# Decoder layer on one Trainium2 core: one block's top-256 found by dropping 128 keys, the embedding norm's affine pass of chunk 1 moved to GpSimd, logits stored with the sign changed

## Chip, cores, metric

One core of one Trainium2 chip. The metric is the device time of one launch in microseconds; of the kernel before there are three timed runs and one profiled execution.

## What is computed

One layer of a decoder over 1024 tokens of width 1024, float32. The parts that matter here:

```python
x = layer_norm(x, emb_ln_g, emb_ln_b)          # gain and bias per column: the affine pass
proj = x @ w_in                                # pool channels 512 | q 512 | latent 128 | indexer q, k, w
pooled = trailing means over 2, 4, 8, 16 tokens, minus the token
score[t, s] = sum_h w[t, h] * relu(iq[t, h] . ik[s]), causal
idx = top_k(score, 256)                        # per token
logits = q_lat . c[idx] / 8 + bias[t - s];  p = softmax(logits) per head
x = layer_norm(2 ** 0.25 * x + concat(pool, attn) @ w_o)
x = layer_norm(2 ** 0.25 * x + relu(x @ w_up) ** 2 @ w_down)
```

The selected keys are not gathered: a mask of 0 (selected) and -1e30 is added to the logits of all keys up to the block's end. The softmax needs the maximum of a row before exp.

## The kernel before

Tokens come in two chunks of 512, each of four blocks of 128. Weights are streamed in units of 128 x 1024 float32 through four ring slots (`wring`); ACT copies each to a rounded part `whi`, GpSimd or DVE subtracts to get `wlo` (`split_lo`, L413), two slots each, and PE multiplies three passes per product. The order of work on each engine is written out by hand, with semaphores; nothing reorders it. PE runs projections of chunk 0, projections of chunk 1, attention 0, output projection 0, feed-forward 0, then attention 1, output projection 1, feed-forward 1. `rows` holds the token rows of one chunk, so the rows of the other chunk wait in DRAM (`spilld`).

**Selection.** Blocks 2 and 3 (384 and 512 keys) are selected together by `select_pair`, on DVE, while PE projects chunk 1: 32 rounds of MAX8 (the eight largest of a row) and MATCH_REPLACE8 (replace them by TAKEN, -3e38), for both blocks in turn. `mask_of` (L878, L879) turns what was taken into the mask. Blocks 0 and 1 have no more than 256 keys. Blocks 4 to 7 are selected later one by one, in feed-forward 0 (`select`, L912 to L919, 640 to 1024 keys).

**Pooling.** `pooling` (L544 to L563) makes four groups of channels from `uT`; in chunk 1 PE's order is q0 q1 q2 u0 u1 u2 po0 u3 po1 q3 po2 po3, and each `po` waits for one group. The last of them is PE's last work before attention 0; GpSimd's head masks for attention 0 wait for it too.

**The affine pass.** `emb_gains` multiplies `rows` by the gain and adds the bias, two passes of 128 x 1024 per block (L656, L657). Chunk 0's is on GpSimd at the start. Chunk 1's is on DVE: three blocks between the groups of pooling, the fourth in step 16 of attention 0. SP then writes the rows to DRAM, loads the next gains, and loads chunk 0's rows for the residual.

**Attention.** A step is one head of one block. DVE adds mask and logits from PSUM and reduces to the row's maximum (L932), negates it (L936), ACT takes exp with that as the bias, PE transposes, ACT and DVE split the transposed probabilities (L948), PE multiplies with the latents. Two buffers alternate between steps.

**Feed-forward 0.** Four groups of 16 units: units 0 to 7 are columns of `w_up`, units 8 to 15 pairs of `w_down` rows. GpSimd does all `wlo` splits, each two units ahead of PE, and in units 0 to 7 the low part of the activations; before its splits at units 11 and 15 it adds four pieces of y to `rows` (`add_y`, L748). SP issues each unit's load when the split of four units earlier is done. Behind feed-forward 0 SP loads four `w_o` units, ACT makes the first two rounded parts at the last two units of the last group, GpSimd makes their low parts after its last `add_y`, and then the head masks of attention 1.

## Time and profile before

| | us |
|---|---|
| runs, median of 3 | 1287.44 (1285.87 to 1287.86) |
| profiled execution, its own time | 1285.83 |
| its span, first to last instruction | 1283.9 |
| PE busy | 1213.2 (94% of the span) |
| DVE busy | 857.3 (67%) |
| ACT busy | 557.8 (43%) |
| GpSimd busy | 494.6 (39%) |
| mean granted clock of TensorE | 0.984 |

A row of the profile names the engine, the line, the operation, `out<-in` and the shapes; in a time order the first number is the start in us from the span's start, the second the duration, and a bracket at the end gives the idle time of the engine before it and what ended that. PE's busy time includes modelled ends of matmuls that overlap. PE is TensorE, DVE VectorE, ACT ScalarE, POOL GpSimd, SP the engine whose queue issues the DMAs.

### The profile page before, as it was taken

The page shows a single profiled execution, that of the slowest core. Times are in us where ns is not written, and L with a number is a line of the kernel's source. Part 1 is how long each engine was busy: PE and PEld are TensorE (multiplying, and loading weights), DVE is VectorE, ACT ScalarE, POOL GpSimd, SP SyncE. Part 2 cuts the span into 40 slices and gives each one's busy share as a digit, 9 for nine tenths or more (in the row PEclk, how much of TensorE's full clock was granted, in tenths as well). Part 3 has the DMA queues.
Part 4 walks back from the last instruction along what each step waited for, and adds up shares of the span by engine and source line. Part 5 has one row for each costly group of instructions (what it writes and reads, how often), then busy time and mean ns, then how long its engine had stood idle before and what let it go on. Part 6 is the DMA issues. An engine that isn't in the chain of part 4 may idle for free.

```text
span 1283.9 us, 17048 instructions
## 1 busy us (share of the span) xinstructions
PE 1213.2 (94%) x5639; PEld 975.5 (76%) x5639; DVE 857.3 (67%) x1326; ACT 557.8 (43%) x943; POOL 494.6 (39%) x362
## 2 busy tenths in 40 slices
PE   4999899699989999999999999989899999999997
PEld 2787686577868878778778779878788888888886
DVE  7677999775966888888888768956532232332336
ACT  3444653576346334344244276662243342442440
POOL 5534674432526666666675652302101101102002
PEclk9899999899989999999999999999899999999999
DMA  6631232031302332233232300224022332333241
GB/s 199 223 98 50 67 98 99 17 148 34 99 17 66 98 99 85 95 98 94 85 98 98 114 2 18 84 98 132 17 95 87 98 98 87 92 98 98 85 127 68
DMA packets 125728, 114.38 MB, mean 89 GB/s; under 512 B 5661, under 2 KB 99434, under 8 KB 125674
## 3 DMA queue, kind: packets, MB, share of 16 engines
q1 hardware_dynamic: 125674, 113.67, 28.7%
q8 instruction: 33, 0.54, 0.2%
q14 instruction: 21, 0.17, 0.0%
HBM read 105.25 MB, written 8.40 MB: 89 GB/s over the span
## 4 chain that ended last, share of the span: by engine, by line
PE 75%; DVE 13%; issue 6%; ACT 2%; POOL 2%; DMA 1%; DVEq 1%; POOLq 0%; SPq 0%; ACTq 0%
PE g_bank L1465 13%; PE g_bank L1467 13%; PE g_bank L1466 13%; PE wide L1465 10%; PE wide L1467 10%; PE wide L1466 10%; PE g_bank L1430 3%; DVE logit L932 1%; DVE score L871 1%; DVE win L548 1%; PE wide L1570 1%; DVE probs_lo L948 1%; DVE work L898 1%; PE wide L1529 1%; PE wide L1530 1%
## 5 line engine op out<-in xcount | busy, mean ns | idle before, releaser
L413 POOL TENSOR_TENSOR wlo<-wring,whi 128x1024 fp32r<-128x1024 f32 (+1 forms) x94 | 230.1, 2449 | 263.3 <-ACT whi L1348 140.8
L1465 PE MATMUL g_bank<-xhi,whi 128*128 128x512 f32 (+1 forms) x736 | 297.3, 404 | 6.1 <-DVE xlo L578 2.7
L1466 PE MATMUL g_bank<-xlo,whi 128*128 128x512 f32 (+1 forms) x736 | 293.1, 398 | 0.0
L1467 PE MATMUL g_bank<-xhi,wlo 128*128 128x512 f32 (+1 forms) x736 | 293.0, 398 | 0.0
L1348 ACT ACTIVATE whi<-wring 128x1024 fp32r<-128x1024 f32 x120 | 127.1, 1059 | 361.7 <-PE g_bank L1467 179.9
L413 DVE TENSOR_TENSOR wlo<-wring,whi 128x1024 fp32r<-128x1024 f32 (+1 forms) x66 | 88.1, 1336 | 218.7 <-ACT whi L1348 217.5
L1465 PE MATMUL wide<-whi,hhi 128*128 128x512 f32 x480 | 190.0, 396 | 0.0
L1466 PE MATMUL wide<-wlo,hhi 128*128 128x512 f32 x480 | 189.6, 395 | 0.0
L1467 PE MATMUL wide<-whi,hlo 128*128 128x512 f32 x480 | 189.6, 395 | 0.0
L1465 PEld LDWEIGHTS g_bank<-xhi,whi 128*128 128x128 f32 (+1 forms) x736 | 138.9, 189 | 45.0 <-issue 5.1
L748 POOL TENSOR_TENSOR rows<-rows,y_stage 128x512 f32<-128x512 f32 x56 | 72.7, 1317 | 249.2 <-ACT y_stage L1338 247.9
L1467 PEld LDWEIGHTS g_bank<-xhi,wlo 128*128 128x128 f32 (+1 forms) x736 | 138.6, 188 | 34.9 <-issue 0.9
L1466 PEld LDWEIGHTS g_bank<-xlo,whi 128*128 128x128 f32 (+1 forms) x736 | 139.1, 189 | 34.1 <-issue 2.0
L916 DVE MAX8 top<-work 128x8 f32<-128x640 f32 (+3 forms) x128 | 131.7, 1029 | 18.7 <-DVE work L919 0.2
L919 DVE MATCH_REPLACE8 work<-top,work 128x640 f32<-128x640 f32 (+3 forms) x128 | 129.2, 1010 | 0.0
L1465 PEld LDWEIGHTS wide<-whi,hhi 128*128 128x128 f32 x480 | 90.0, 187 | 23.0 <-POOL wlo L413 1.2
L1467 PEld LDWEIGHTS wide<-whi,hlo 128*128 128x128 f32 x480 | 90.0, 187 | 22.1
L1466 PEld LDWEIGHTS wide<-wlo,hhi 128*128 128x128 f32 x480 | 90.0, 187 | 21.8
L1161 ACT ACTIVATE whi<-wring 128x1024 fp32r<-128x1024 f32 (+1 forms) x40 | 41.6, 1041 | 118.3 <-PE g_bank L1467 104.0
L739 POOL TENSOR_TENSOR mask<-score,near_bias 128x256 f32<-128x256 f32 (+1 forms) x64 | 44.7, 700 | 78.4 <-DVE row_max L932 68.5
L871 DVE SCALAR_TENSOR_TENSOR score<-relu_sb,idx_w,score 128x384 f32<-128x384 f32 (+5 forms) x42 | 56.7, 1363 | 27.1 <-ACT relu_sb L1227 26.0
L932 DVE CUSTOM_DVE_ANT_0 logit<-wide,mask 128x128 f32<-128x128 f32 (+7 forms) x64 | 48.3, 755 | 31.6 <-PE g_bank L1430 25.5
(200 smaller groups left out, 1932.3 us busy)
## 6 DMA issues: line engine op xcount, KB each, us to landing
wring<-in_w_up SPq DMA_DIRECT2D x64, 512.0 KB, 4.0
wring<-in_w_down SPq DMA_DIRECT2D x64, 512.0 KB, 3.7
wring<-in_w_in SPq DMA_DIRECT2D x26, 512.0 KB, 3.7
wring<-in_w_o SPq DMA_DIRECT2D x16, 512.0 KB, 3.7
rows<-in_x SPq DMA_DIRECT2D x8, 512.0 KB, 5.2
normalized_rows<-rows SPq DMA_DIRECT2D x8, 512.0 KB, 4.0
rows<-normalized_rows SPq DMA_DIRECT2D x8, 512.0 KB, 6.6
out<-rows SPq DMA_DIRECT2D x7, 512.0 KB, 2.6
```

The lines of the kernel that those rows point to most:

```text
L413: eng.tensor_tensor(parts_of(name, lo_tile(name)), parts_of(name, wring[n % 4]), parts_of(name, hi_tile(name)).bitcast(F32), ALU.subtract) ...
L739: pool.tensor_tensor(mask[:, m % 2, length - near:length], score[:, i % CB, length - near:length], near_bias[:, h, NEAR - near:NEAR], ALU. ...
L748: pool.tensor_tensor(piece, piece, y_stage[:, b, :], ALU.add).then_inc(y_added, 1)
L871: nc.vector.scalar_tensor_tensor(out=s, in0=relu_sb[:, n % 2, 0:length], scalar=idx_w[:, i, h:h + 1], in1=s, op0=ALU.mult, op1=ALU.add)\
L916: nc.vector.max(top8[:, 0, :], w).then_inc(topk_steps, 1)
L919: nc.vector.match_replace(w, top8[:, 0, :], w, TAKEN).then_inc(topk_steps, 1)
L932: nc.vector.tensor_tensor_reduce(logit[:, m % 2, 0:length], wide[m % 2][:, 0:length], mask[:, m % 2, 0:length], 1.0, TAKEN, ALU.add, ALU.m ...
L1161: nc.scalar.activation(parts_of(name, hi_tile(name)), parts_of(name, wring[n % 4]), ACT.Copy).then_inc(hi_ready, 1)
L1348: nc.scalar.activation(whi[(R[("mlp", c, 0)] + j) % 2][:, :], wring[(first + j + 2) % 4][:, :], ACT.Copy)\
L1465: nc.tensor.matmul(out_ap, w_hi, m_hi, start=first, stop=False)
L1466: nc.tensor.matmul(out_ap, w_hi, m_lo, start=False, stop=False)
L1467: return nc.tensor.matmul(out_ap, w_lo, m_hi, start=False, stop=last)
```

## The change

Three parts; none changes what is computed.

1. `select_pair`: block 2 has 384 keys, of which 256 are selected, so 128 are dropped. Its scores are copied negated and in reverse order of keys, 16 rounds take the 128 smallest, and one operation turns those into the mask. Block 3 goes on alone for 16 more rounds. In `pooling` a scaling and a subtraction become one operation.
2. The affine pass of chunk 1 leaves DVE. SP writes the normalized rows to DRAM at once; during feed-forward 0 it loads one block per group into `emb_stage` (which lies, with `emb_rows_g`, where the indexer keys and two parked `w_o` units have been), GpSimd makes the two passes on it before its split at unit 13, and SP writes the block back. The loops over groups of SP and GpSimd in feed-forward 0 are written out.
3. The masked logits are stored negated, `-(logit + mask)`, with a running minimum, which is the negated maximum itself; exp gets the scale -1.

```diff
         key_lo = part("key_lo", 100.25, [P, S], F32R)
+        emb_rows_g = part("emb_rows_g", 88.25, [P, 2, D])
...
                 sp.wait_ge(*LO[units[first - 1]])
+                    with sp.Fori(0, GROUPS) as g:
+                        for j in range(GUNITS):
+                            load_mlp_unit(c, g, j)
+                    return
+                for g in range(GROUPS):
                     for j in range(GUNITS):
...
+                        load_mlp_unit(c, g, j)
+                        if (g, j) == (0, 8):
+
+                            sp.wait_ge(proj_full, 2 * CB)
+                            sp.wait_ge(relu_ready, 48)
+                            sp.dma_start(emb_rows_g[:, 0, :], emb_ln_g.rearrange("(o d) -> o d", o=1).to_broadcast([P, D])).then_inc(emb_gain_in, 16)
+                            sp.dma_start(emb_rows_g[:, 1, :], emb_ln_b.rearrange("(o d) -> o d", o=1).to_broadcast([P, D])).then_inc(emb_gain_in, 16)
+                        if j == 8:
+                            load_stage(g)
+                        if j == 4 and g:
+                            store_stage(g - 1)
+                store_stage(CB - 1)
+
+            def load_stage(b):
+
+                sp.wait_ge(spilled, 16 * (NB + max(b - 1, 0)))
+                sp.dma_start(emb_stage[:, b % 2, :], spilld[CB + b]).then_inc(stage_in, 16)
+
+            def store_stage(b):
+
+                sp.wait_ge(emb_rows, CB + b + 1)
+                sp.dma_start(spilld[CB + b], emb_stage[:, b % 2, :]).then_inc(spilled, 16)
...
             for b in range(CB):
-                sp.wait_ge(emb_rows, CB + b + 1)
+                sp.wait_ge(xhat_ready, CB + b + 1)
                 sp.dma_start(spilld[CB + b], rows[:, b, :]).then_inc(spilled, 16)
+            sp.wait_ge(emb_rows, CB)
             load_gains(ln1_g, ln1_b)
             sp.wait_ge(spilled, 16 * NB)
+
+            sp.wait_ge(g_full, EV[("xT", 1, KT - 1)])
             for b in range(CB):
                 sp.dma_start(rows[:, b, :], spilld[b]).then_inc(rows_in, 16)
             load_units(units[U[("wo", 0, 1, 0)]:U[("mlp", 0, 0)]])
...
             sp.wait_ge(stored, 16 * CB)
+            sp.wait_ge(spilled, 16 * (NB + CB))
             for b in range(CB):
                 sp.dma_start(rows[:, b, :], spilld[CB + b]).then_inc(rows_in, 16)
...
                 if g >= 2:
 
                     eng.wait_ge(g_full, EV[("po", c, g - 2)])
-                link(eng.tensor_scalar(done, src[:, HIST:HIST + CHUNK], 1.0 / w, None, ALU.mult))
                 if c == 0:
 
                     link(eng.tensor_tensor(done[:, 0:w - 1], src[:, HIST:HIST + w - 1], recip_count[:, 0:w - 1], ALU.mult))
                     link(eng.tensor_copy(hist[:, g, :], u[:, CHUNK:CHUNK + HIST]))
-                eng.tensor_tensor(done, done, u[:, HIST:HIST + CHUNK], ALU.subtract).then_inc(pooled_ready, 1)
+                    link(eng.tensor_tensor(done[:, 0:w - 1], done[:, 0:w - 1], u[:, HIST:HIST + w - 1], ALU.subtract))
+                at = w - 1 if c == 0 else 0
+                eng.scalar_tensor_tensor(out=done[:, at:CHUNK], in0=src[:, HIST + at:HIST + CHUNK], scalar=1.0 / w,
+                                         in1=u[:, HIST + at:HIST + CHUNK], op0=ALU.mult, op1=ALU.subtract)\
+                    .then_inc(pooled_ready, 1)
...
+            def emb_gains():
+
+                pool.wait_ge(gains_in, 32)
+                pool.wait_ge(g_full, EV[("xT", 0, KT - 1)])
+                for b in range(CB):
+                    link(pool.tensor_tensor(rows[:, b, :], rows[:, b, :], gains[:, 0, :], ALU.mult))
+                    pool.tensor_tensor(rows[:, b, :], rows[:, b, :], gains[:, 1, :], ALU.add).then_inc(emb_rows, 1)
+
+            def staged_gains(b):
+
+                pool.wait_ge(emb_gain_in, 32)
+                pool.wait_ge(stage_in, 16 * (b + 1))
+                row = emb_stage[:, b % 2, :]
+                link(pool.tensor_tensor(row, row, emb_rows_g[:, 0, :], ALU.mult))
+                pool.tensor_tensor(row, row, emb_rows_g[:, 1, :], ALU.add).then_inc(emb_rows, 1)
...
                     if j in (GT + 3, GT + 7):
                         add_y(c, g, (j - GT) // 4)
+                    if j == GT + 5:
+                        staged_gains(g)
...
-            mlp_lo(pool, 0, 0, False, first_group)
-            with pool.Fori(1, GROUPS - 1) as g:
-                mlp_lo(pool, 0, g, False, add_at(0, g))
-            mlp_lo(pool, 0, GROUPS - 1, True, add_at(0, GROUPS - 1))
+            for g in range(GROUPS):
+                mlp_lo(pool, 0, g, g == GROUPS - 1, first_group if g == 0 else add_at(0, g))
...
             def select_pair():
 
                 w = [work[:, 0:3 * P], work[:, 3 * P:7 * P]]
+                drop, rounds = P // 8, TOPK // 8
 
                 dve.wait_ge(diag_masked, 2)
-                for e in range(2):
-                    nc.vector.tensor_copy(w[e], score[:, 2 + e, 0:(3 + e) * P]).then_inc(topk_steps, 1)
-                with dve.Fori(0, TOPK // 8) as r:
+                nc.vector.tensor_scalar(w[0], score[:, 2, 3 * P - 1::-1], -1.0, None, ALU.mult).then_inc(topk_steps, 1)
+                nc.vector.tensor_copy(w[1], score[:, 3, 0:4 * P]).then_inc(topk_steps, 1)
+                with dve.Fori(0, drop) as r:
                     for e in range(2):
 
                         dve.wait_ge(topk_steps, 4 * r + (1 + e))
@@ -896,9 +947,19 @@
                         dve.wait_ge(topk_steps, 4 * r + (3 + e))
                         dve.sem_inc(topk_turn, 1)
                         nc.vector.match_replace(w[e], top8[:, e, :], w[e], TAKEN).then_inc(topk_steps, 1)
-                dve.wait_ge(topk_steps, 2 + 4 * (TOPK // 8))
-                for e in range(2):
-                    mask_of(2 + e, w[e])
+
+                dve.wait_ge(topk_steps, 2 + 4 * drop)
+                s = score[:, 2, 3 * P - 1::-1]
+                nc.vector.tensor_scalar(s, w[0], TAKEN, NEG, ALU.is_equal, ALU.mult).then_inc(mask_ready, 1)
+                with dve.Fori(0, rounds - drop) as r:
+                    dve.wait_ge(topk_steps, 2 * r + (2 + 4 * drop))
+                    dve.sem_inc(topk_turn, 1)
+                    nc.vector.max(top8[:, 1, :], w[1]).then_inc(topk_steps, 1)
+                    dve.wait_ge(topk_steps, 2 * r + (3 + 4 * drop))
+                    dve.sem_inc(topk_turn, 1)
+                    nc.vector.match_replace(w[1], top8[:, 1, :], w[1], TAKEN).then_inc(topk_steps, 1)
+                dve.wait_ge(topk_steps, PAIR_STEPS)
+                mask_of(3, w[1])
...
                 nc.vector.tensor_tensor_reduce(logit[:, m % 2, 0:length], wide[m % 2][:, 0:length],
-                                               mask[:, m % 2, 0:length], 1.0, TAKEN, ALU.add, ALU.max,
-                                               row_max[:, m % 2:m % 2 + 1]).then_inc(masked, 1)
-                dve.wait_ge(masked, m + 1)
-                nc.vector.tensor_scalar(neg_max[:, m % 2:m % 2 + 1], row_max[:, m % 2:m % 2 + 1], -1.0, None,
-                                        ALU.mult).then_inc(neg_max_ready, 1)
+                                               mask[:, m % 2, 0:length], -1.0, -TAKEN, ALU.add, ALU.min,
+                                               neg_max[:, m % 2:m % 2 + 1]).then_inc(masked, 1)
...
                         mask_logits(step)
-                    if step == 16:
-
-                        next(gained)
...
             select_pair()
-            gained = emb_gains(dve, 1, chain)
             for g in pooling(dve, 1, chain):
-                if g < 3:
-                    next(gained)
+                pass
             dve.wait_ge(masks01_ready, 2)
             attention(0)
...
-                act.wait_ge(neg_max_ready, m + 1)
+                act.wait_ge(masked, m + 1)
                 p = logit[:, m % 2, 0:(i + 1) * P]
-                nc.scalar.activation(p, p, ACT.Exp, bias=neg_max[:, m % 2:m % 2 + 1],
+                nc.scalar.activation(p, p, ACT.Exp, scale=-1.0, bias=neg_max[:, m % 2:m % 2 + 1],
                                      accum_out=exp_sum[:, i % 2, h:h + 1]).then_inc(exp_ready, 1)
...
             act.wait_ge(y_added, CB + 8 * GROUPS)
+
+            act.wait_ge(spilled, 16 * (NB + CB))
             attention(1)
```

DVE from the selection to the second group of pooling in chunk 1 (`win` is a partial window sum), before:

```order
L898 MATCH_REPLACE work<-top,work 128x512
L888 REGISTER_ALU
L888 COMPARE_AND_BRANCH
L878 TENSOR_TENSOR score<-work,score 128x384
L879 TENSOR_SCALAR score<-score 128x384
L878 TENSOR_TENSOR score<-work,score 128x512
L879 TENSOR_SCALAR score<-score 128x512
L544 COPY uT<-hist 128x16
L548 TENSOR_TENSOR win<-uT 128x527
L558 TENSOR_SCALAR pooledT<-win 128x512
L563 TENSOR_TENSOR pooledT<-pooledT,uT 128x512
L656 TENSOR_TENSOR rows<-rows,gains 128x1024
```

and after the change, from the end of the paired loop:

```order
L939 COMPARE_AND_BRANCH
L953 TENSOR_SCALAR score<-work 128x384
L954 UNCONDITIONAL_BRANCH
L954 ISA
L957 MAX top<-work 128x8
L958 REGISTER_ALU
L960 MATCH_REPLACE work<-top,work 128x512
L954 REGISTER_ALU
L954 COMPARE_AND_BRANCH
L928 TENSOR_TENSOR score<-work,score 128x512
L929 TENSOR_SCALAR score<-score 128x512
L582 COPY uT<-hist 128x16
```

A second loop of 512 keys alone has come in, and the passes on `rows` that stood between the groups are gone.

POOL in the second half of a group of feed-forward 0 after the change (L415 are the splits, L797 the additions of y, L788 and L789 the staged passes):

```order
L797 TENSOR_TENSOR rows<-rows,y_stage 128x512 x4
L415 TENSOR_TENSOR wlo<-wring,whi 128x1024 x2
L788 TENSOR_TENSOR emb_stage<-emb_stage,emb_rows_g 128x1024
L789 TENSOR_TENSOR emb_stage<-emb_stage,emb_rows_g 128x1024
L415 TENSOR_TENSOR wlo<-wring,whi 128x1024 x2
L797 TENSOR_TENSOR rows<-rows,y_stage 128x512 x4
```

Before, four splits stood between the two sets of additions, with nothing among them.

SP at the end of feed-forward 0 after the change:

```order
L499 DMA wring3<-in_w_down 128x2x512 [waits lo_pool]
L483 DMA normalized_rows<-emb_stage_117 128x1024 [waits emb_rows]
L437 DMA wring0<-in_w_o 128x2x512 [waits lo_pool]
L437 DMA wring1<-in_w_o 128x2x512 [waits lo_pool]
L437 DMA wring2<-in_w_o 128x2x512 [waits lo_pool]
L437 DMA wring3<-in_w_o 128x2x512 [waits lo_pool]
```

The store with its wait for GpSimd's last staged pass is new; the loads of `w_o` stood right behind the last unit's load.

## Rows read from the trace of the kernel before

**Rows 1.** Busy us (x instructions) of each engine in a stretch, granted clock, DMA share, GB/s

```profile
core 0: us, PE busy (x) PEld busy (x) DVE busy (x) ACT busy (x) POOL busy (x), PEclk, DMA share, GB/s
...
203.00:234.00 31.00, 20.19 (x79) 14.15 (x78) 29.79 (x37) 8.06 (x11) 11.40 (x4) 0.88 0.27 95
...
365.00:738.00 373.00, 373.00 (x1606) 299.46 (x1604) 310.13 (x417) 152.32 (x210) 231.72 (x129) 1.00 0.29 90
...
768.00:857.00 89.00, 83.66 (x607) 76.45 (x605) 72.48 (x145) 57.62 (x125) 21.56 (x33) 1.00 0.19 72
```

**Rows 2.** Waits of PE, 200 to 236 us: total, times, longest

```profile
PE g_bank L1551 <- DVE pooledT L563: 9.1, 2, 8.2
```

**Rows 3.** The chain of waits, 120 to 262 us: start, duration, what

```profile
203.82 0.43 DVE score L879
...
233.81 2.09 PE g_bank L1551 x2
```

**Rows 4.** DVE in order of time, 120 to 260 us

```profile
130.40 1.14 DVE L893 MAX8 top<-work 128x8 f32<-128x384 f32 x2
...
199.85 1.16 DVE L893 MAX8 top<-work 128x8 f32<-128x384 f32 x2
...
210.78 2.37 DVE L544 COPY uT<-hist 128x16 f32<-128x16 f32 x1
...
224.30 3.37 DVE L656 TENSOR_TENSOR rows<-rows,gains 128x1024 f32<-128x1024 f32 x1
...
228.84 0.17 DVE L544 COPY uT<-hist 128x16 f32<-128x16 f32 x1
```

**Rows 5.** DVE in the rounds of block 4 (640 keys)

```profile
408.10 0.83 DVE L916 MAX8 top<-work 128x8 f32<-128x640 f32 x1
...
410.13 0.83 DVE L916 MAX8 top<-work 128x8 f32<-128x640 f32 x1 [0.15 <-DVE work L919]
```

**Rows 6.** ACT and POOL in order of time, at the last group of pooling

```profile
216.30 0.58 ACT L1128 ACTIVATE uT<-g_bank 128x512 f32<-128x512 f32 x1
...
216.47 2.94 POOL L413 TENSOR_TENSOR wlo<-wring,whi 128x1024 fp32r<-128x1024 f32 x1 [3.35 <-ACT whi L1161]
```

**Rows 7.** POOL, DVE and ACT in a group of feed-forward 0

```profile
542.63 2.41 POOL L413 TENSOR_TENSOR wlo<-wring,whi 128x1024 fp32r<-128x1024 f32 x1 [1.32 <-ACT whi L1348]
548.40 3.20 POOL L413 TENSOR_TENSOR wlo<-wring,whi 128x1024 fp32r<-128x1024 f32 x1 [3.36 <-ACT whi L1348]
...
548.38 0.96 DVE L878 TENSOR_TENSOR score<-work,score 128x768 f32<-128x768 f32 x1
...
552.94 1.06 ACT L1348 ACTIVATE whi<-wring 128x1024 fp32r<-128x1024 f32 x1 [4.62 <-PE wide L1467]
```

**Rows 8.** PE in order of time, step 16 of attention 0

```profile
258.79 0.52 PE L1430 MATMUL g_bank<-ident,logit 128*128 128x128 f32 x3 [1.71 <-DVE probs_lo L948]
```

**Rows 9.** DVE and ACT in order of time, first step of attention 0

```profile
236.82 0.08 DVE L932 DVE_READ_ACCUMULATOR2_ANT row_max<- 128x1 f32 x1
236.94 0.15 DVE L936 TENSOR_SCALAR neg_max<-row_max 128x1 f32<-128x1 f32 x1
...
237.13 0.40 ACT L1259 ACTIVATE logit<-logit,neg_max 128x128 f32<-128x128 f32 x1 [0.53 <-DVE neg_max L936]
```

**Rows 10.** The chain of waits in both attentions: pieces of the negation

```profile
236.94 0.17 DVE neg_max L936
...
850.46 0.15 DVE neg_max L936
```

**Rows 11.** DVE: the first mask operation at the end of three selections

```profile
472.28 2.27 DVE L878 TENSOR_TENSOR score<-work,score 128x640 f32<-128x640 f32 x1
...
633.92 2.08 DVE L878 TENSOR_TENSOR score<-work,score 128x896 f32<-128x896 f32 x1
...
727.18 1.22 DVE L878 TENSOR_TENSOR score<-work,score 128x1024 f32<-128x1024 f32 x1
```

**Rows 12.** ACT at the end of feed-forward 0; landing of a burst of four loads

```profile
732.90 1.06 ACT L1161 ACTIVATE whi<-wring 128x1024 fp32r<-128x1024 f32 x1 [4.62 <-PE wide L1467]
...
DMA to landing us min/median/max: 5.1/6.5/8.8
```

More of the change, by code:

```diff
@@ L299, in layer @@
         emb_rows = sem("emb_rows")
+        emb_gain_in = sem("emb_gain_in")
+        stage_in = sem("stage_in")
         x1_rows = sem("x1_rows")
@@ new lines, in load_mlp, with load_mlp_unit @@
+                store_stage(CB - 1)
[5 more added lines that the diff above has]
+                sp.dma_start(spilld[CB + b], emb_stage[:, b % 2, :]).then_inc(spilled, 16)
+            def load_mlp_unit(c, g, j):
+                first = U[("mlp", c, 0)]
+                sem_lo, lo_base = LO[("mlp", c, 0)]
+                slot = (first + j) % 4
+                sp.wait_ge(sem_lo, g * GUNITS + (lo_base - 1 + j - 4 + 1))
+                if j < GT:
+                    src = wupd[:, :, bass.ds(g * (GT * P) + j * P, P)]
+                    dst = k_columns(wring[slot])
+                else:
+                    nh, u = divmod(j - GT, 4)
+                    src = wdownd[:, bass.ds(g * GT + 2 * u, 2), nh * 512:nh * 512 + 512]
+                    dst = k_pairs(wring[slot])
+                sp.dma_start(dst, src).then_inc(ring_in[slot], 16)
@@ L649, in mlp_lo @@
                         .then_inc(h_lo_ready[c], 1)
-        def emb_gains(eng, c, link):
-            eng.wait_ge(gains_in, 32)
-            eng.wait_ge(g_full, EV[("xT", c, KT - 1)])
-            for b in range(CB):
-                link(eng.tensor_tensor(rows[:, b, :], rows[:, b, :], gains[:, 0, :], ALU.mult))
-                eng.tensor_tensor(rows[:, b, :], rows[:, b, :], gains[:, 1, :], ALU.add).then_inc(emb_rows, 1)
-                yield b
         @block.gpsimd
@@ L754, in _ @@
             inverse_std(EMB0)
-            for b in emb_gains(pool, 0, link):
-                pass
+            emb_gains()
             latents_inverse_rms(0)
@@ L908, in select @@
                 rounds = TOPK // 8
-                first = 2 + 4 * rounds + (2 * rounds + 1) * (i - 4)
+                first = PAIR_STEPS + (2 * rounds + 1) * (i - 4)
                 dve.wait_ge(diag_masked, i - 1)
```

16 lines of the change are left out of this document (3 added, 13 removed).

## Prediction

> **What bounds the kernel now.** I read the busy time by stretches first [rows 1]. From 365 to 738 us (chunk 0's feed-forward) PE is busy for all 373 us: nothing taken off another engine shortens it, and only something that makes PE wait can change it. Time can be gained where PE has holes: 203 to 234 us (20.19 busy of 31, granted clock 0.88) and the attentions. Busy time overstates PE in the attentions, since the ends of matmuls are modelled and short ones overlap, so there I go by the chain and not by the busy share.
>
> The waits of PE name the first hole: 9.1 us for `pooledT`, 8.2 of it in one piece [rows 2]. The chain gives the order of events: the pair's selection ends with a mask operation at 203.82 + 0.43, and the last pool product (two matmuls) starts at 233.81, takes 2.09 us at the clock that had fallen behind the hole, and opens attention 0 [rows 3]. DVE's order of time shows what lies between: the selection runs from 130.40, its last round starts at 199.85 (31 rounds in 69.45 us, 2.24 each), and then pooling alternates with the gain and bias passes on `rows`. Two DVE operations there are far longer than their size: the gain pass of 3.37 us at 224.30, and a copy of 16 columns that takes 2.37 us at 210.78 and 0.17 at 228.84 [rows 4]. The long ones met a split on GpSimd.
>
> **The selection.** The first 16 rounds stay pairs: 16 x 2.24 = 35.8 us. The other 16 handle 512 keys alone. No row shows a round of 512 alone. From above it is bounded by the round of 640, 410.13 - 408.10 = 2.03 us [rows 5], from below by half of a pair round, 1.12. A fifth of the elements of MAX8 (0.83) and of the equally long replacement goes, 0.33, so I take 1.70: it has the same two waits as the 640 round. Sum 27.2. The two first operations (before: until 130.40) I leave as they are; a reversed read can cost or save there, by at most the 4 us that they take together. With some 0.5 for one mask and 1.1 for the other the selection ends at 130.4 + 35.8 + 27.2 + 1.6 = 195.0 instead of 204.2, 9 us earlier (4 to 18).
>
> **Pooling of chunk 1.** Its last group needs `u3`, which ACT writes from 216.30 to 216.88; GpSimd started a split at 216.47 [rows 6], and the copy into `uT` waits for its end as the one at 210.78 did: with the 2.4 of an undisturbed split [rows 7], until 218.9. Then the group itself: from 228.84 [rows 4] to 233.81 it took 4.97, of which one pass over 512 (some 0.5) is fused away: 4.5. The product can start at 218.9 + 4.5 = 223.4, against 233.81: 10.4 earlier, and without a hole of 8 us PE stays at 2.4 GHz instead of 1.2, so it takes about 1.1 instead of 2.09. **Term A: -11.4** (-9.5 to -13). Selection and passes don't add. With the passes gone, DVE pools three groups and idles before `u3` even if the selection ended at 204.2. With the passes kept and the selection short, the last pass would still hide mostly in this same slack. The dropped rounds thus buy slack rather than time, and an error in my round of 1.70 costs nothing up to 8 us.
>
> **The passes in attention 0.** The fourth block's two passes stand in step 16, and behind them PE idles 1.71 us for `probs_lo` [rows 8]; loops around it lose a little too. **Term B: -1.9** (0 to -3).
>
> **The sign change.** Before: the accumulator is read from 236.82 to 236.90, the negation follows at 236.94 and takes 0.15, exp starts at 237.13 [rows 9]. With exp behind the read directly, at the 0.04 that it now has behind the negation, 0.19 of latency goes per head step. It counts where the negation is on the chain: 8 pieces in 234 to 298 us and 10 in 747 to 862, the first and the last of the 18 in [rows 10]. **Term C: -18 x 0.19 = -3.4** (-0.5 if neighbouring paths are as long, -8 if DVE's own time counts in the second attention too). I price the main instruction with scale -1 and min like the one before, having no row of it.
>
> **The staged passes in the feed-forward.** This is work that PE could come to wait for. GpSimd's split 14 runs from 542.63 to 545.04 and split 15 starts at 548.40 [rows 7]. Two passes over 1024 columns, priced as splits, 2.4 each, do not fit into 3.36 us: 545.04 + 4.9 = 549.9, and split 15 ends at 552.3. PE needs it when unit 14 ends, which is when ACT's next split starts, 552.94. Margin 0.6 us, where nothing else is in the way. But DVE starts an operation with two SBUF inputs in this gap, the mask at 548.38, and beside it the split took 3.20 instead of 2.40 [rows 7]. The groups are alike and some 90 us apart, so I look where each selection ends [rows 11]. In the second group the mask of 0.96 gets between: 0.96 - 0.6 = 0.4 over the margin. In the third the mask at 633.92 lasts to 636.0, 0.9 into the gap, and its scaling and the next copy (0.6 and 0.7 by their sizes) follow: 2.2 - 0.6 = 1.6. In the fourth the mask at 727.18 takes 1.22 and its scaling 0.6: 1.2. In the first the mask comes at 472.28, outside. **Term D: +3.1** (0 to +6).
>
> The Trainium skill (SBUF — State Buffer, Who interferes with whom) says that the pair of ports shared by DVE and GpSimd is held for a whole instruction by whichever starts first, and that a DVE instruction with two SBUF inputs contends with a GpSimd one that reads SBUF. By it, if GpSimd's second pass always starts before the waiting DVE operation, D would be 0 and the sum 3.1 less; the disturbed rows agree with the lock, none shows who wins between two GpSimd passes.
>
> **The queue of SP.** Its four added loads, four stores and two gain loads fall into the feed-forward, where a weight load is issued four units ahead; the earlier spill and reload of `rows` likewise come long before their use. I price these at nothing, by the cover of four units of 548.40 - 542.63 = 5.8 us [rows 7]. One is different: the store of stage 3 now stands ahead of the four loads of `w_o`. It waits for the fourth staged pass, which by the pattern above ends 3.0 before unit 14 does (732.90 here [rows 12]) and 1.2 later for the mask: at about 731.1. With half a us for the issue of the store, the first `w_o` unit lands at 731.6 + 5.1 = 736.7 or later, by the fastest of a burst of four (5.1/6.5/8.8 us, [rows 12]). ACT wants it at 732.90, or 1.2 later with D, and waits 2.6 us. Queued behind that are the evacuations of y, two of which are paced by PE anyway; GpSimd's additions, its two splits and the first masks of attention 1 come behind them. ACT catches up, GpSimd does not quite. **Term E: +1.0** (0 to +4).
>
> **Sum.** -11.4 - 1.9 - 3.4 + 3.1 + 1.0 = -12.6. The profiled execution would go from 1285.83 to 1273.2 (span 1271.3). The median lies 1.6 above it; I subtract the same from it: 1287.44 - 12.6 = **1274.8 us**. A measurement tells 0.2%, 2.6 us, from no change.
>
> **Rivals.**
> 1. *The staged passes always fit, and GpSimd is late nowhere*: D and E are 0. For it: 0.6 of margin and GpSimd's idle time of 3.3 us. Against: the mask in the gap. 1287.4 - 16.7 = 1270.7. Chance 0.27.
> 2. *DVE's own time counts throughout attention 1*: C is 8, not 3.4. For it: DVE is busy 72.48 of 89 us there [rows 1]. 1274.8 - 4.6 = 1270.2. Chance 0.12.
> 3. *The selection does not shorten as thought, because reversed access is slow*: only beyond 8 us does it reach PE. With 8 us spare and 12 lost it would be 1278.8. Chance 0.04.
> 4. *The other side: the staged passes throw GpSimd out of step in each group.* If both passes and the splits behind them wait for DVE throughout, split 15 is late by the whole 4.9, and the cost decides the sign from 3.9 us per group on (12.6 + 3.1 over four groups): 4 x 4.9 = 19.6 instead of D, 1274.8 + 16.5 = 1291.3. For it: no cover but 3.36 us. Against: DVE's selection rounds in this stage don't lengthen splits. Chance 0.04.
>
> My forecast has the remaining 0.53. Range: from 1268.5 (rival 1 with A 2.2 better) to 1280.5 (C at 0.8 and D and E together 3.1 dearer: -12.6 + 2.6 + 3.1 = -6.9). Rival 4 and several worst ends together lie outside. Faster 0.93, same 0.03, slower 0.04.
>
> **What would show it.** The last pool product near 223.4; DVE idle before it, with the selection ended by 196; ACT's exp 0.04 behind the accumulator read; no DVE pass in attention 0; splits of GpSimd behind the staged passes ending 0 to 1.6 us after PE wants them; the first `w_o` split of ACT some 3 us behind the end of unit 14. It is wrong if PE stops for over 2 us in any group of the feed-forward, if the pool product comes after 226, or if attention 1 begins with a hole much longer than before.

## The result, and the profile after

| | before | changed |
|---|---|---|
| median of the runs side by side, us | 1287.57 (4 runs, 1285.87 to 1287.86) | 1273.15 (4 runs, 1271.55 to 1274.00) |
| ratio, 95% interval | | 0.989, 0.9878 to 0.9902 |
| profiled execution, us (span) | 1285.83 (1283.9) | 1274.00 (1272.2) |

The change brings 14.4 us by the medians; 1274.8 us was predicted, which was a change of 12.6. The profiled executions differ by 11.8, the spans by 11.7. That gap between 14.4 and 11.7 matters below.

The stretches of [rows 1] in the kernel after, the last two moved to where the same work now lies:

```profile
core 0: us, PE busy (x) PEld busy (x) DVE busy (x) ACT busy (x) POOL busy (x), PEclk, DMA share, GB/s
203.00:234.00 31.00, 28.55 (x123) 21.66 (x122) 19.84 (x46) 15.02 (x40) 14.81 (x15) 0.94 0.69 252
353.00:726.00 373.00, 372.29 (x1602) 298.93 (x1601) 315.04 (x417) 151.15 (x209) 248.75 (x134) 1.00 0.32 100
757.00:846.00 89.00, 85.22 (x625) 78.60 (x624) 71.70 (x126) 59.78 (x129) 21.66 (x33) 1.00 0.19 72
```

PE has 28.55 us of work in the first stretch instead of 20.19 and DVE 10 less; in the feed-forward PE loses 0.7; GpSimd carries 17 us more there. The waits of PE from 200 to 236 us, where [rows 2] showed 9.1:

```profile
PE wide L1625 <- DVE neg_max L993: 1.5, 1, 1.5
PE g_bank L1606 <- DVE pooledT L602: 0.7, 1, 0.7
```

DVE, GpSimd and PE around the last pooling group (order of time; they answer to rows 3, 4 and 6):

```profile
196.18 0.43 DVE L929 TENSOR_SCALAR score<-score 128x512 f32<-128x512 f32 x1
...
199.23 1.98 DVE L582 COPY uT<-hist 128x16 f32<-128x16 f32 x1 [2.62 <-ACT uT L1181]
...
216.45 2.41 POOL L415 TENSOR_TENSOR wlo<-wring,whi 128x1024 fp32r<-128x1024 f32 x1 [4.06 <-ACT whi L1214]
...
216.89 2.00 DVE L582 COPY uT<-hist 128x16 f32<-128x16 f32 x1 [1.13 <-ACT uT L1181]
...
222.47 0.69 DVE L602 SCALAR_TENSOR_TENSOR pooledT<-win,uT 128x512 f32<-128x512 f32 x1
...
222.90 2.47 POOL L415 TENSOR_TENSOR wlo<-wring,whi 128x1024 fp32r<-128x1024 f32 x1 [4.05 <-ACT whi L1214]
...
223.21 1.12 PE L1606 MATMUL g_bank<-pooledT,poolw 128*128 128x512 f32 x2 [0.69 <-DVE pooledT L602]
...
225.32 0.86 POOL L772 TENSOR_TENSOR mask<-score,near_bias 128x128 f32<-128x128 f32 x2
...
225.96 0.29 DVE L993 CUSTOM_DVE_ANT_0 logit<-wide,mask 128x128 f32<-128x128 f32 x1 [2.80 <-POOL mask L772]
```

The last pool product starts at 223.21 (223.4 predicted) and at full clock. The selection ends at 196.6 (195.0 predicted) and DVE then idles 2.62 us for `u0`: the slack is there. What I had not looked at comes after the product: GpSimd's split of 222.90 stands ahead of the first two head masks, so DVE reads the first logits at 225.96. Without that split the first logits come 0.9 earlier (c_all below).

**Stage by stage.** PE executes the same 5639 matmuls in the same order in both kernels. So I took the start of one and the same matmul in two traces, subtracted, and noted how that difference grows from stage to stage. All figures of this kind below are worked out from the starts in the traces. The kernel before minus the changed kernel, us:

| stretch (times of the changed kernel) | before loses there | forecast |
|---|---|---|
| start to 200 | -0.3 | 0 |
| 200 to 226: last pool product, first logits | +11.0 | A 11.4 |
| 226 to 282: attention 0 | +2.3 | B 1.9, and part of C |
| 282 to 290: entry of the projection | -1.6 | 0 |
| 290 to 365 | +0.4 | 0 |
| 365 to 735: feed-forward 0 | -0.6 | D -3.1 |
| 735 to 738: entry of attention 1 | -1.0 | E -1.0 |
| 738 to 845: attention 1 | +3.1 | part of C |
| 845 to the end | -1.6 | 0 |
| sum | 11.7 | 12.6 |

The two entries of -1.6 have nothing to do with the change. The granted clock shows them, here in the profiled execution of the changed kernel, and below in a second submission of the very same kernel (a_again), whose work at 277 to 285 is that of 281 to 289 here. The row of 226 to 232 shows a third such stretch, hidden in the +2.3 (the one at 846 a_again met as well):

```profile
130.00:146.00 16.00, 12.53 (x54) 7.87 (x53) 16.00 (x44) 11.27 (x18) 10.24 (x8) 0.79 0.13 34
226.00:232.00 6.00, 5.45 (x26) 4.62 (x27) 3.25 (x19) 4.71 (x21) 3.57 (x8) 0.72 0.96 359
281.00:289.00 8.00, 6.55 (x26) 5.42 (x27) 4.63 (x9) 4.01 (x8) 0.00 (x0) 0.79 0.01 2
846.00:854.00 8.00, 6.27 (x30) 5.20 (x29) 3.20 (x6) 3.55 (x7) 0.00 (x0) 0.79 0.00 1
```

```profile
130.00:146.00 16.00, 12.53 (x59) 8.28 (x58) 16.00 (x45) 12.68 (x19) 10.78 (x9) 0.89 0.12 34
226.00:232.00 6.00, 5.79 (x38) 4.79 (x38) 3.57 (x21) 5.58 (x25) 3.97 (x7) 1.00 0.84 312
277.00:285.00 8.00, 6.27 (x36) 5.20 (x36) 5.42 (x11) 5.23 (x11) 0.00 (x0) 1.00 0.01 2
```

At the same place of the same kernel PE ran a part of the matmuls at 1.2 GHz in one execution (mean 0.79 at 281 to 289) and all at 2.4 in the other (1.00). The stretch at 226 to 232 cost the changed kernel 1.1 us: a_again, at full clock there, gains just that on it between 228 and 232. The kernel before was at 1.00 where it does the work of the two -1.6 entries (292 to 300 and 857 to 865 us of its own time), and the clock that had fallen in its hole (0.50 from 228 to 234) was up again when its first logits came (0.94 from 236 to 242). Without the three stretches, which the kernel before did not meet, the profiled executions would differ by 11.7 + 1.6 + 1.6 + 1.1 = 16.0. The medians say 14.4 in this submission and 17.2 in that of a_again (1287.25 and 1270.03 below).

The Trainium skill (TensorE: Matmul & The Clock Gate, Part 1) says of a kernel's first matmuls that the number of slow ones varies from run to run of the same kernel; these rows show the same for stretches in the middle of one.

### The profile page after: what moved, and what is told of

Read it like the earlier page. It is cut to its first block, busy times and chain, and to the rows that moved or that the text cites. A ratio compares the mean times of both kernels' runs of the same rounds, so it can differ in the third digit from the quotient of the medians.

```text
span 1272.2 us, 16625 instructions
## 1 busy us (share of the span) xinstructions
PE 1212.9 (95%) x5639; PEld 978.5 (77%) x5639; DVE 830.0 (65%) x1201; ACT 557.6 (44%) x943; POOL 511.9 (40%) x370
## 4 chain that ended last, share of the span: by engine, by line
PE 82%; POOL 7%; DVE 5%; issue 2%; ACT 2%; DMA 1%; POOLq 0%; DVEq 0%; SPq 0%; ACTq 0%
PE g_bank L1520 16%; PE g_bank L1521 16%; PE g_bank L1522 16%; PE wide L1520 8%; PE wide L1522 8%; PE wide L1521 8%; PE g_bank L1485 4%; POOL wlo L415 3%; POOL rows L797 2%; PE wide L1625 1%; PE wide L1584 1%; PE wide L1585 1%; PE g_bank L1672 1%; DVE probs_lo L1006 1%; POOL emb_stage L789 1%
## 5 line engine op out<-in xcount | busy, mean ns | idle before, releaser
L415 POOL TENSOR_TENSOR wlo<-wring,whi 128x1024 fp32r<-128x1024 f32 (+1 forms) x94 | 228.7, 2434 | 249.2 <-ACT whi L1214 126.0
L415 DVE TENSOR_TENSOR wlo<-wring,whi 128x1024 fp32r<-128x1024 f32 (+1 forms) x66 | 88.3, 1339 | 218.6 <-ACT whi L1401 217.6
L797 POOL TENSOR_TENSOR rows<-rows,y_stage 128x512 f32<-128x512 f32 x56 | 72.5, 1318 | 249.6 <-ACT y_stage L1391 248.6
```

Source lines behind the costliest of these rows:

```text
L415: eng.tensor_tensor(parts_of(name, lo_tile(name)), parts_of(name, wring[n % 4]), parts_of(name, hi_tile(name)).bitcast(F32), ALU.subtract) ...
L797: pool.tensor_tensor(piece, piece, y_stage[:, b, :], ALU.add).then_inc(y_added, 1)
```

## The experiments

Twelve kernels ran in three submissions, each on a chip of its own: b_sel, a_fullsel, a_neg and a_dvepass in the first, c_nostage, c_wofirst, c_spread and a_nofuse in the second, the other four in the third. The kernel before stood at 1287.20, 1286.89 and 1287.25 beside them. In the table each is compared with the changed kernel's profiled execution, as above (positive: that much later), since two medians of the changed kernel turned out 3 us apart. "To 226" is taken at the first matmuls behind the first logits; a matmul sooner or later moves an entry there by up to 0.2.

| kernel | median us | to 200 | to 226 | to 282 | to 290 | to 365 | to 735 | to 738 | to 845 | to end |
|---|---|---|---|---|---|---|---|---|---|---|
| b_sel | 1282.83 | 0.0 | +7.6 | +2.2 | -1.6 | +0.6 | -0.7 | -1.0 | +3.2 | -1.5 |
| a_fullsel | 1270.97 | -1.5 | 0.0 | -1.1 | -1.6 | +0.4 | 0.0 | +0.2 | 0.0 | +0.2 |
| a_neg | 1275.85 | -0.5 | 0.0 | +0.7 | -1.6 | -0.3 | 0.0 | -0.1 | +3.1 | +0.1 |
| a_dvepass | 1277.71 | -2.0 | +5.5 | +0.5 | -1.6 | +0.7 | -0.5 | +0.1 | +0.4 | +0.1 |
| c_nostage | 1271.05 | +0.2 | 0.0 | -0.5 | -1.6 | +0.4 | -0.9 | +0.5 | 0.0 | -1.0 |
| c_wofirst | 1269.84 | +0.2 | 0.0 | -0.4 | -1.6 | +0.4 | 0.0 | -1.0 | 0.0 | -1.7 |
| c_spread | 1270.89 | +0.6 | 0.0 | 0.0 | 0.0 | 0.0 | -0.8 | -1.0 | 0.0 | -1.6 |
| a_nofuse | 1273.76 | -0.1 | +2.8 | -1.0 | -1.6 | -0.2 | 0.0 | -0.1 | 0.0 | 0.0 |
| a_again | 1270.03 | -1.6 | 0.0 | -1.1 | -1.6 | +0.3 | 0.0 | -0.2 | 0.0 | -1.1 |
| c_all | 1271.15 | -0.1 | -0.9 | -1.1 | -0.1 | +0.3 | -0.3 | +0.2 | 0.0 | +0.3 |
| c_all_full | 1271.21 | +0.4 | -0.9 | -1.1 | -0.1 | +0.4 | -0.8 | +0.5 | 0.0 | -1.1 |
| c_all2 | 1267.59 | -0.5 | -1.4 | 0.0 | 0.0 | 0.0 | -0.5 | +0.1 | 0.0 | +0.3 |

The row of a_again is the yardstick: it is the changed kernel, so whatever it shows is no effect of an edit. It is within 0.2 where PE is kept busy or waits for a fixed chain, and -1.1 or -1.6 where the clock had dropped in the one execution and not in the other. A difference of up to 1.6 in the columns "to 200", "to 290", "to 365" and "to end" is therefore not read, and one in "to 282" only from 232 us on, where all executions ran at full clock until 281, or with the 1.1 of the clock taken off.

### The selection: b_sel and a_fullsel

b_sel is the kernel before with the new `select_pair` (and `PAIR_STEPS` in `select`) and nothing else:

```diff
-                with dve.Fori(0, TOPK // 8) as r:
+                with dve.Fori(0, drop) as r:
...
+                with dve.Fori(0, rounds - drop) as r:
```

> The kernel before with the new selection of blocks 2 and 3 alone; the passes, the pooling and the negation stay as they were. Prediction's view (the last pass hides in the slack behind u3): selection ends near 196, last pool product near 224.5 instead of 233.81, time 10 us lower, about 1277.5. Rival 'one for one' (DVE has no slack while it carries the passes, so it gives back just what the selection saves): 29.6 us from the end of the selection to the product as before, product at 226.2, 7.6 to 8.5 us lower, about 1279.5. Rival 'the selection is worth nothing by itself': 1287.

Measured 1282.83, ratio 0.9972 (0.996 to 0.9985): 4.4 us, so the prediction's view (10 us) is wrong, and the time lies between the two rivals: half of what 'one for one' gave, and not nothing. DVE at both ends of the pooling, and the product:

```profile
196.20 0.43 DVE L881 TENSOR_SCALAR score<-score 128x512 f32<-128x512 f32 x1
199.25 1.98 DVE L544 COPY uT<-hist 128x16 f32<-128x16 f32 x1 [2.62 <-ACT uT L1141]
...
229.94 0.69 DVE L563 TENSOR_TENSOR pooledT<-pooledT,uT 128x512 f32<-128x512 f32 x1
...
230.69 2.07 PE L1564 MATMUL g_bank<-pooledT,poolw 128*128 128x512 f32 x2 [8.14 <-DVE pooledT L563]
```

The selection ends 7.6 us earlier than in [rows 3], but 2.62 of that is lost at once: `u0` is not there before 199.25. From there DVE never waits again, the three passes stand in its way as before, and the hole of 8.14 and the low clock behind it stay. It brings 3.4 at the first logits (11.0 - 7.6). Nearly all of that is won at the second and third pool products, which come 1.0 and 1.9 earlier: there PE had waited for `pooledT` and `qT` and no longer does.

a_fullsel is the reverse, the changed kernel with all 32 pair rounds:

```diff
-                with dve.Fori(0, drop) as r:
+                with dve.Fori(0, TOPK // 8) as r:
```

> The changed kernel with all 32 pair rounds for blocks 2 and 3 again. Prediction's view (with the passes gone the rounds buy slack, up to 8 us): selection ends near 204.7, the pooling groups of 4.5 us end at about 223 to 224.5, last pool product at most 1 us later than 223.21, time 1273.2 to 1274.2. Rival 'one for one': product near 231, 1281.

Measured 1270.97, ratio to before 0.9875 (0.9859 to 0.9892). Of the 8 us of added rounds none reaches PE:

```profile
202.67 0.43 DVE L927 TENSOR_SCALAR score<-score 128x512 f32<-128x512 f32 x1
203.02 2.37 DVE L582 COPY uT<-hist 128x16 f32<-128x16 f32 x1
...
221.01 0.69 DVE L602 SCALAR_TENSOR_TENSOR pooledT<-win,uT 128x512 f32<-128x512 f32 x1
...
221.76 1.12 PE L1593 MATMUL g_bank<-pooledT,poolw 128*128 128x512 f32 x2 [0.69 <-DVE pooledT L602]
```

PE waits the same 0.69 us for the same operation; the start of 221.76 instead of 223.21 is all inherited from before 200 us. The pooling starts 3.8 us later in the trace (5.2 measured against PE, which runs 1.45 ahead) and has caught up by the last group. The line of a_fullsel in the table equals that of a_again within 0.5 in every stretch up to 845. So beside the other edits the dropped rounds are worth nothing, within 0.1 us at the pool product.

### The passes: a_dvepass

The changed kernel with the four affine passes of chunk 1 on DVE as before, and nothing staged:

```diff
             for g in pooling(dve, 1, chain):
-                pass
+                if g < 3:
+                    next(gained)
```

> The changed kernel with the affine passes of chunk 1 back on DVE where they stood (three between the pooling groups, one in attention 0) and nothing staged in the feed-forward. Prediction's view: the last pass hides behind u3 (0 to 1 us), the pass in attention 0 costs 1.9, and the 1.7 us that the trace after shows lost in the feed-forward and at the start of attention 1 come back: 1273.2 to 1274.5. Rival 'one for one': last pool product near 226.2 instead of 223.2, so 3.0 + 1.9 - 1.7 = 3.2 us slower, 1276.4.

Measured 1277.71, ratio 0.9928 (0.9911 to 0.9944). The product comes 3.3 later by the traces, and since this execution was 2.0 ahead at 200 us, 5.3 is lost there (5.5 at the first logits), so both theories were too small. DVE shows why:

```profile
208.94 3.29 DVE L658 TENSOR_TENSOR rows<-rows,gains 128x1024 f32<-128x1024 f32 x1
...
214.97 2.78 DVE L562 SCALAR_TENSOR_TENSOR pooledT<-win,uT 128x512 f32<-128x512 f32 x1
217.66 1.21 DVE L657 TENSOR_TENSOR rows<-rows,gains 128x1024 f32<-128x1024 f32 x1
218.91 1.22 DVE L658 TENSOR_TENSOR rows<-rows,gains 128x1024 f32<-128x1024 f32 x1
...
221.19 2.62 DVE L546 TENSOR_TENSOR win<-win 128x526 f32<-128x526 f32 x1
...
226.47 2.08 PE L1562 MATMUL g_bank<-pooledT,poolw 128*128 128x512 f32 x2 [5.93 <-DVE pooledT L562]
```

The pass does not hide: it ends at 220.1, when `u3` has long been there. And each GpSimd split now catches some DVE operation at its start, which then takes about 2 us more (2.78 for one of 0.69). In attention 0 this kernel loses 1.6 between 245 and 266, where its fourth pass stands. That is term B by itself; the +0.5 in the table is this less the 1.1 that the clock cost the changed kernel.

The traces also split the 11.0 of the last pool product and first logits, along one order of the edits: from the kernel before to b_sel 3.4 (the selection), from b_sel to a_dvepass 2.1 (7.6 - 5.5, the fusion; the sign change, also in it, moves nothing here by a_neg's 0.0), from a_dvepass to the changed kernel 5.5 (the passes). In another order the shares differ: taken out last, the selection is worth 0.

### Fusing the scaling: a_nofuse

```diff
-                eng.scalar_tensor_tensor(out=done[:, at:CHUNK], in0=src[:, HIST + at:HIST + CHUNK], scalar=1.0 / w,
-                                         in1=u[:, HIST + at:HIST + CHUNK], op0=ALU.mult, op1=ALU.subtract)\
+                link(eng.tensor_scalar(done, src[:, HIST:HIST + CHUNK], 1.0 / w, None, ALU.mult))
...
+                eng.tensor_tensor(done, done, u[:, HIST:HIST + CHUNK], ALU.subtract).then_inc(pooled_ready, 1)
```

> The changed kernel with pooling's scaling and subtraction as two operations again. Prediction: each group 0.5 us longer, of which the last counts: last pool product at 223.7 instead of 223.2, 0.5 us slower, 1273.7. Rival 'it moves nothing, PE has 0.7 of hole only and other work stands behind': 0.

Measured 1273.76, ratio 0.9905 (0.9887 to 0.9923). That is 0.6 above the changed kernel's 1273.15, as if the forecast had held, but the median hides it: the first logits come 2.8 later, not 0.5.

```profile
222.35 0.43 DVE L596 TENSOR_SCALAR pooledT<-win 128x512 f32<-128x512 f32 x1
222.81 2.85 DVE L601 TENSOR_TENSOR pooledT<-pooledT,uT 128x512 f32<-128x512 f32 x1
...
222.77 2.34 POOL L415 TENSOR_TENSOR wlo<-wring,whi 128x1024 fp32r<-128x1024 f32 x1 [4.05 <-ACT whi L1211]
...
225.71 2.08 PE L1603 MATMUL g_bank<-pooledT,poolw 128*128 128x512 f32 x2 [3.31 <-DVE pooledT L601]
```

GpSimd's split starts at 222.77, the subtraction at 222.81, 0.04 too late, and it waits for the whole split. In the changed kernel the fused operation starts at 222.47, 0.43 ahead of the split, and takes 0.69. The fusion saves its own 0.45 and keeps the last operation out of the collision; what follows (a longer hole, product at 2.08 instead of 1.12) is paid too.

### The sign change: a_neg

```diff
-                                               mask[:, m % 2, 0:length], -1.0, -TAKEN, ALU.add, ALU.min,
+                                               mask[:, m % 2, 0:length], 1.0, TAKEN, ALU.add, ALU.max,
...
+                nc.vector.tensor_scalar(neg_max[:, m % 2:m % 2 + 1], row_max[:, m % 2:m % 2 + 1], -1.0, None,
```

> The changed kernel with logits of the old sign and the negation between maximum and exp again. Prediction's term C: 18 chain pieces of 0.19, 3.4 us slower, 1276.6, most of it in attention 1. Rival 'DVE's own time counts throughout attention 1': 8 us slower, 1281. Rival 'neighbouring paths are as long': 0.5 us, 1273.7.

Measured 1275.85, ratio 0.9918 (0.9901 to 0.9934): 2.7 above the changed kernel's 1273.15, but in another submission. By the starts it loses 3.1 in attention 1. In attention 0 the table's 0.7 is too small, since the clock had dropped in both executions (0.72 granted from 226 to 232 in each) but over different work: from 232 us on, with both at full clock, a_neg loses 1.0, and before that 0.2 by the first transpose behind an exp. A second way gives more: kernel before minus changed kernel 2.3, plus the clock's 1.1, less 1.6 for the pass, is 1.8. So attention 0 is worth 1.2 to 1.8, and the sign change 4.3 to 4.9 in all. The latency per step is as priced. In the changed kernel, first step of attention 0, exp follows the read directly:

```profile
226.18 0.08 DVE L993 DVE_READ_ACCUMULATOR2_ANT neg_max<- 128x1 f32 x1
...
226.30 0.40 ACT L1312 ACTIVATE logit<-logit,neg_max 128x128 f32<-128x128 f32 x1 [1.24 <-DVE neg_max L993]
```

From the start of the read to exp it is 0.12, in [rows 9] 0.31: 0.19 less.

### The staged passes: c_nostage, c_spread, c_wofirst

c_nostage leaves the two GpSimd passes out (chunk 1's residual then has neither gain nor bias):

```diff
-                link(pool.tensor_tensor(row, row, emb_rows_g[:, 0, :], ALU.mult))
-                pool.tensor_tensor(row, row, emb_rows_g[:, 1, :], ALU.add).then_inc(emb_rows, 1)
+                pool.sem_inc(emb_rows, 1)
```

> The changed kernel with the two GpSimd passes on the staged rows left out (loads, stores and waits stay; chunk 1's residual gets neither gain nor bias). Measures what the passes cost. Prediction's terms D and E: 4.1 us less, 1269.1. Theory from the trace after (PE loses 0.5 in the second group, 0.6 in the third, nothing in the first and fourth, and 0.6 at the start of attention 1): 1.7 us less, 1271.4, with no PE wait for a split in the feed-forward. Rival 'they cost nothing': 1273.2.

c_spread puts one pass in each of two gaps, earlier in the group:

```diff
-                    if j == GT + 5:
-                        staged_gains(g)
+                    if j in (GT + 1, GT + 2):
+                        staged_gains(g, j - GT - 1)
```

> The changed kernel with the staged gain pass before split 11 and the bias pass before split 12 of each group (one pass of 2.4 us in each of two idle gaps of 3.2 us) instead of both before split 15. Theory 'two passes in one gap collide': nothing is late, and the fourth pass no longer holds up the w_o loads, 1.7 us less, 1271.4, like the kernel without passes. Rival 'the passes take DVE's port time wherever they stand': as after, 1273.2.

c_wofirst moves `store_stage(CB - 1)` behind the loads of `w_o`:

```diff
-                store_stage(CB - 1)
...
             load_units(units[U[("wo", 1, 0, 0)]:U[("wo", 1, 1, 0)]])
+            store_stage(CB - 1)
```

> The changed kernel with the store of stage 3 behind the four w_o loads in SP's queue instead of ahead of them. Prediction's term E: ACT's first w_o split 2.6 us earlier, 1.0 us less, 1272.2. Theory from the trace after: 0.6 less in attention 1's start, 1272.5. Rival 'the additions of y are paced by PE anyway': 0, 1273.2.

Measured 1271.05, 1270.89 and 1269.84 (ratios 0.9882, 0.9877 and 0.9863, each within 0.0025 to either side). In the feed-forward c_nostage gains 0.9 and c_spread 0.8, c_wofirst nothing; at the entry of attention 1 c_spread and c_wofirst gain 1.0 each (c_nostage's clock was down there, 0.5 lost, though the step of 0.9 for the store is in its trace too). That is far from the 4.1 that D and E together would have given. So the passes cost 0.8 in the feed-forward, spreading them removes that, and the store costs 1.0. The changed kernel's third group shows the collision, GpSimd first, then DVE:

```profile
623.50 2.38 POOL L788 TENSOR_TENSOR emb_stage<-emb_stage,emb_rows_g 128x1024 f32<-128x1024 f32 x1
625.96 3.13 POOL L789 TENSOR_TENSOR emb_stage<-emb_stage,emb_rows_g 128x1024 f32<-128x1024 f32 x1
629.04 2.78 POOL L415 TENSOR_TENSOR wlo<-wring,whi 128x1024 fp32r<-128x1024 f32 x1
...
623.56 3.27 DVE L928 TENSOR_TENSOR score<-work,score 128x896 f32<-128x896 f32 x1
626.86 2.71 DVE L929 TENSOR_SCALAR score<-score 128x896 f32<-128x896 f32 x1
629.49 2.88 DVE L973 COPY work<-score 128x1024 f32<-128x1024 f32 x1
...
631.44 1.06 ACT L1401 ACTIVATE whi<-wring 128x1024 fp32r<-128x1024 f32 x1 [4.61 <-PE wide L1522]
```

The engines take turns. DVE's mask waits for the first pass, runs at some 625.9, the second pass waits for it (3.13 instead of 2.40), DVE's scaling waits for that one, and so on. Split 15 ends at 631.82; PE wanted it when ACT's next split starts, 631.44. Here is 0.6 of the 0.7 of PE's waits. In the second group split 15 ends at 541.23, with nothing to spare before 541.24, and PE's next product is late too. Against c_nostage PE loses 0.8 in the third group and 0.4 in the second at this point and regains 0.25 later in each. In the first and fourth DVE is in its rounds, all fits, and PE loses nothing.

The store, SP and ACT in the changed kernel, then in c_wofirst:

```profile
719.00 0.34 SPq L483 DMA_DIRECT2D normalized_rows<-emb_stage  x1
719.38 2.39 SPq L437 DMA_DIRECT2D wring<-in_w_o  x4
...
724.54 1.06 ACT L1214 ACTIVATE whi<-wring 128x1024 fp32r<-128x1024 f32 x1 [7.22 <-DMA wring<-in_w_o]
```

```profile
719.92 0.37 SPq L437 DMA_DIRECT2D wring<-in_w_o  x1
720.33 0.47 SPq L482 DMA_DIRECT2D normalized_rows<-emb_stage  x1
...
720.50 1.06 ACT L1214 ACTIVATE whi<-wring 128x1024 fp32r<-128x1024 f32 x1 [4.62 <-PE wide L1522]
```

With c_wofirst 1.45 ahead at this point, ACT's split comes 2.6 earlier by its own doing (4.04 - 1.45), and PE gains 1.0 of it.

### The same kernel again, and versions with less in the way

c_all is c_spread plus the split of the second `w_o` unit on DVE behind the last pooling group; c_all_full is that with 32 pair rounds; c_all2 puts the first `w_o` unit's split on DVE too:

```diff
             for g in pooling(dve, 1, chain):
-                pass
+                if g == 2:
+                    split_lo(dve, ("wo", 0, 0, 0), lo_dve)
+            split_lo(dve, ("wo", 0, 0, 1), lo_dve)
             dve.wait_ge(masks01_ready, 2)
```

> The changed kernel once more, beside the variants below. Every theory: 1273.2, within 1; the selection cut is worth nothing here if this is no faster than the kernel with full selection, 1271.0.

> The changed kernel with the staged passes spread over two gaps and the split of the second w_o unit on DVE behind its last pooling group instead of on GpSimd. Theory: 1.7 from the passes, and GpSimd's first masks of attention 0 start right behind the last pool product (near 224.3 instead of 225.32), so the first logits come 1.1 earlier: 2.8 less, 1270.4. Rival 'the split on DVE delays the last pooling group or the first logits itself': 1271.5.

> The same as the kernel with both, but with all 32 pair rounds. Theory 'the cut rounds are slack': the same time, within 0.5, and every PE position behind 200 us equal but for the clock. Rival 'the cut is worth its 8 us partly': 1 us or more slower.

> As the kernel with both, and the split of the first w_o unit on DVE too, between pooling groups 2 and 3, so that the last group never meets a GpSimd split. Theory 'the lock makes the copy wait 1.8 of its 2.0 us': DVE pays 1.3 for the split and saves 1.8, PE's 0.7 hole before the last pool product shrinks to 0.2: 0.5 less, 1269.9. Rival 'DVE's own 1.3 comes on top': 0.7 more.

Measured in one submission: a_again 1270.03 (0.9875, 0.9857 to 0.9894), c_all 1271.15 (0.9876, 0.986 to 0.9893), c_all_full 1271.21 (0.988, 0.9864 to 0.9896), c_all2 1267.59 (0.985, 0.9835 to 0.9866). The changed kernel's own median thus moved by 3.1 from one submission to the next, which were on different chips; the kernel before stayed within 0.7. By the starts c_all gains 0.9 at the first logits and 0.7 in the feed-forward up to 720, but meets the low clock at 732 and gains nothing at the entry of attention 1. c_all_full equals c_all at the logits: the cut is worth nothing here either. c_all2's last pooling group meets no split:

```profile
215.88 1.23 DVE L415 TENSOR_TENSOR wlo<-wring,whi 128x1024 fp32r<-128x1024 f32 x1 [0.65 <-ACT whi L1218]
...
217.03 0.17 DVE L582 COPY uT<-hist 128x16 f32<-128x16 f32 x1
...
220.78 0.69 DVE L602 SCALAR_TENSOR_TENSOR pooledT<-win,uT 128x512 f32<-128x512 f32 x1
...
220.99 1.88 PE L1610 MATMUL g_bank<-pooledT,poolw 128*128 128x512 f32 x4
```

The copy takes 0.17 instead of 2.00, PE's hole of 0.69 before the last product is gone (the last two pool products run as one, x4), and the first logits come 1.4 earlier. c_all2 has the lowest median of all. Its interval still touches that of a_again, so that it beats the changed kernel is likely by the stages (1.4 and 0.5 gained) and not settled by the times.

## Why the prediction was right

**Term A** (11.4 forecast, 11.0 measured) rested on the last pool product, and each link held: copy behind the split, group of 4.5, product at full clock. That the clock then stays up was not so in the profiled execution: it fell at the first logits (0.72 from 226 to 232), behind holes of 0.69 and 1.53 us only, and that cost 1.1 us; in a_again it did not fall. The selection came 1.6 late, though its rounds began 1.1 early: a single round takes 1.74 instead of 1.70, and the mask of block 2 met a split (2.18 instead of 0.5). As the prediction said, an error there costs nothing, and a_fullsel shows that even all 8 us cost nothing. One sentence of it was wrong: "with the passes kept and the selection short, the last pass would still hide mostly". a_dvepass loses 5.3 at the product, and b_sel brings 3.4 instead of the 10 that followed from this sentence. It did not enter the sum.

The fusion was priced at 0.5 within A. It is worth 2.8 in place, since without it the last operation starts 0.04 behind a split. That the forecast came out right here was luck: 4.5 per group put that operation ahead of the split, but I had not seen the split: its start at 222.9 was never compared with the end of the group.

**Term B** (1.9) measured 1.6. **Term C** (3.4) was too small; it measured 4.3 to 4.9 at equal clock. In attention 0 the 8 chain pieces gave 1.5, as measured (1.2 to 1.8). In attention 1 the 10 pieces gave 1.9 and 3.1 was measured: over 32 steps that is 0.1 per step, half of the 0.19, so more steps counted than stood on the chain of the old trace. Rival 2 (8 us) does not hold, though it named the right attention.

**Term D** (3.1) is the term that was mis-sized most; measured 0.8. I added up every DVE operation that the old trace had in or near the gap (0.4, 1.6 and 1.2). In group 2 the forecast 0.4 was there, less 0.25 regained. In group 3 only part of the queue got in ahead of split 15, since the DVE operations also had to wait their turn. In group 4 the mask no longer fell into the gap. It stood at 727.18 before [rows 11], and PE is some 11 us earlier there, yet it now starts at 722.29, well behind split 15: each DVE operation that waited for a pass in groups 2 and 3 had delayed DVE's rounds. A collision shifts the next one; I had left DVE's schedule fixed. Rival 1, which set both D and E to 0, was nearer on D than the forecast, but not on E, and rival 4 (GpSimd out of step in each group) is refuted by the ends of split 15.

The rule of the Trainium skill (SBUF — State Buffer, Who interferes with whom) that the port pair is held for a whole instruction agrees with the rows shown here, such as 2.00 for a copy of 16 columns that takes 0.17. The case it left open for the prediction, two GpSimd instructions in a row with a DVE one waiting, these rows answer: DVE got in between (rows at 625.96 and 629.04).

**Term E** (1.0) measured 1.0, with the 2.6 us of ACT's lateness as forecast.

Measured by stage the terms make 11.0 + 1.6 + (4.3 to 4.9) - 0.8 - 1.0 = 15.1 to 15.7, against 12.6 forecast and 14.4 and 17.2 by the medians of two submissions. Of the 2.5 to 3.1 us that were missed, 2.3 are D and 0.9 to 1.5 are C, both on the same side, less 0.7 from A and B. That the profiled spans differ by 11.7 only is the clock at 228, 282 and 850 us. So the nearness of the profiled execution (1274.00) to its forecast (1273.2) is partly luck: the 2.5 to 3.1 that the terms missed and the 4.3 that the clock took from this execution and not from the one before went opposite ways.

## What to carry to other kernels

Two edits that shorten the same engine's stretch don't add: find what arrives last when the engine is free (here `u3` and PE itself), and keep only the edit that gets there. Where DVE and GpSimd both work in SBUF, compare the start of the next GpSimd instruction with the start of the last DVE one on the path: 0.04 us on the wrong side cost 2.8. When effects are near 0.2% of the time, compare the starts of the same matmul in two traces stage by stage, with a rerun of the same kernel as yardstick, before a median is believed.

## What the runs showed of the hardware

- One kernel, two submissions: medians 1273.15 and 1270.03, spans of the profiled executions 1272.2 and 1267.0 at mean granted clocks of 0.984 and 0.988. Nearly the whole difference lies where PE has holes (130 to 146, 226 to 232, 281 to 289 us and behind 899), in which stretches ran at 1.2 or at 2.4 GHz by turns: 1.6, 1.1, 1.6 and 1.2 us.
- A reversed read costs nothing visible: the first operation on 384 reversed columns took 1.55 us and the copy of 512 behind it 2.58, together 4.13, where before the two forward copies took 4.05.
- The min with scale -1 takes as long as the max with scale 1: 0.29 us at 128 columns and 0.82 to 0.83 at 640, in both kernels.
